# A scan kernel's chunk products on four quarters of the matmul array, with its state products and its levels issued by shape

## The reference, cut to what matters

```
def step(s, inp):
    r_t, w_t, k_t, v_t, kk_t, a_t = inp
    sa = jnp.einsum('bhvk,bhk->bhv', s, -kk_t)
    s = (s * w_t[:, :, None, :] + sa[..., None] * (kk_t * a_t)[:, :, None, :]
         + v_t[..., None] * k_t[:, :, None, :])
    return s, jnp.einsum('bhvk,bhk->bhv', s, r_t)
```

## Time and profile before

| | |
|---|---|
| median of 3 runs | 4100.36 us (4093.78 to 4100.76) |
| the profiled execution, its own time | 4094.72 us |
| its span, first to last instruction | 4092.9 us |
| mean granted clock of TensorE | 0.943 of full |
| the scan, from its first to its last instruction on PE | about 1131 to 2293 us |
| bodies with a solve and state steps, between starts of `begin0` | 17, from 1183 to 2253 us |

### The profile page before, as it was taken

The page is one execution under the profiler, slowest core; times in us unless marked ns, Lnnn a source line. Parts: engine busy times, 40 slices in busy tenths (PEclk is TensorE's granted clock), DMA queues, the critical chain, the costliest instruction groups (busy, mean ns, idle before and its releaser), DMA issues. The chain is left out here.

```text
span 4092.9 us, 93137 instructions
## 1 busy us (share of the span) xinstructions
PE 3684.4 (90%) x39677; PEld 3199.6 (78%) x39677; DVE 2350.2 (57%) x4331; ACT 1910.5 (47%) x2991; POOL 1215.6 (30%) x1222
## 2 busy tenths in 40 slices
PE   5699999999978898988989688897599999999997
PEld 2578888888767777777778588675499999999986
DVE  3236666640046766766667655343666666667676
ACT  3335666641145665665656444232244443444454
POOL 1223333331045555555553255101001010111102
PEclk7799999999989999999999799898699999999999
DMA  5235555542264454444442466343367676666786
GB/s 172 62 120 176 179 180 169 176 148 75 69 127 87 94 107 82 91 106 86 96 85 47 155 217 188 119 145 122 101 203 213 205 212 205 201 216 206 235 278 218
DMA packets 771394, 611.33 MB, mean 149 GB/s; under 512 B 267618, under 2 KB 698532, under 8 KB 769956
## 3 DMA queue, kind: packets, MB, share of 16 engines
q1 hardware_dynamic: 721828, 493.84, 42.2%
q0 software_dynamic: 22688, 80.75, 6.6%
q10 hardware_dynamic: 26464, 30.77, 2.5%
HBM read 443.62 MB, written 161.50 MB: 148 GB/s over the span
## 5 line engine op out<-in xcount | busy, mean ns | idle before, releaser
L579 PE MATMUL moe_h<-moe_xt_hi,moe_w_hi 128*128 128x256 f32 x2048 | 583.2, 285 | 7.9 <-DVE moe_w_lo L431 4.0
L431 DVE TENSOR_TENSOR moe_w_lo<-moe_w_lo_whole,moe_w_hi 128x2048 fp32r<-128x2048 f32 x254 | 446.3, 1757 | 243.4 <-ACT moe_w_hi L647 196.5
L579 PE MATMUL moe_h<-moe_xt_hi,moe_w_lo 128*128 128x256 f32 x2048 | 580.9, 284 | 0.0
L579 PE MATMUL moe_h<-moe_xt_lo,moe_w_hi 128*128 128x256 f32 x2048 | 580.9, 284 | 0.0
L1963 PE MATMUL inward_pp<-u_u_hi,inward_w_hi 128*128 128x512 f32 (+1 forms) x1360 | 527.9, 388 | 20.4 <-POOL inward_w_lo L2123 20.4
L1963 PE MATMUL inward_pp<-u_u_lo,inward_w_hi 128*128 128x512 f32 (+1 forms) x1360 | 516.3, 380 | 0.0
L1963 PE MATMUL inward_pp<-u_u_hi,inward_w_lo 128*128 128x512 f32 (+1 forms) x1360 | 516.0, 379 | 0.0
L579 PEld LDWEIGHTS moe_h<-moe_xt_hi,moe_w_hi 128*128 128x128 f32 x2048 | 394.1, 192 | 19.0 <-issue 5.9
L579 PEld LDWEIGHTS moe_h<-moe_xt_lo,moe_w_hi 128*128 128x128 f32 x2048 | 394.2, 192 | 3.6
L579 PEld LDWEIGHTS moe_h<-moe_xt_hi,moe_w_lo 128*128 128x128 f32 x2048 | 394.1, 192 | 0.0
L487 POOL DMA_INDIRECT scratch_x<-moe_ys,moe_who x30 | 86.1, 2870 | 867.0 <-DVE moe_ys L753 748.5
(11 more groups left out here) (386 smaller groups left out, 8929.7 us busy)
## 6 DMA issues: line engine op xcount, KB each, us to landing
moe_w_lo_whole<-in_moe_w SPq DMA_DIRECT2D x384, 512.0 KB, 5.1
scratch_ops<-inward_ops SPq DMA_DIRECT2D x72, 512.0 KB, 3.8
scan_by_parity<-scratch_ops SPq DMA_DIRECT2D x144, 192.0 KB, 6.4
inward_w_lo_whole<-in_w_in SPq DMA_DIRECT2D x38, 512.0 KB, 4.5
scan_aq<-scratch_ops SPq DMA_DIRECT2D x72, 256.0 KB, 4.9
scan_kb<-scratch_ops SPq DMA_DIRECT2D x36, 512.0 KB, 5.7
scratch_gates<-inward_out SPq DMA_DIRECT2D x64, 256.0 KB, 2.1
all_late<-in_w_mod POOLq DMA_DIRECT2D x32, 512.0 KB, 5.2
```

The source lines that it names most:

```text
L431: return nc.vector.tensor_tensor(x_lo, x, x_hi.bitcast(F32), ALU.subtract)
L579: mm = nc.tensor.matmul(hb[ft % 2][m][:, 0:CAP], w_, x_, start=(k == 0 and part == 0), stop=(k == KD - 1 and part == 2))
```

## The change

Four parts, all of the scan or of what feeds it.

1. **Products with B and K.** In `begin1` pair 0's products with B and pair 1's with K are issued in turn (`joint`), in `begin2` the other two. B's go from partitions h to output partitions h, K's from h to the other half, from a copy `over` of K, A and Q with the heads of a pair swapped, so that four matmuls of 64 rows by 64 columns lie on four quarters. `begin2` waits until DVE has taken out both products of `begin1`.
2. **State S.** K's products for both pairs and directions, then Q's, then B's, where before each direction of each pair had its own K, Q, B.
3. **Levels.** The products of both pairs, then the transpositions of both, where before pair 0 had both first.
4. **Layout.** A and Q of a chunk lie side by side in `ops`, with the decays behind, so that one transfer for each pair loads all that was three; `kb` is now `ob` (B alone), and `over` is loaded too, by two transfers for each pair. The decay is a column of this tile, and DVE multiplies by it one direction at a time (two TENSOR_SCALAR instructions for one TENSOR_TENSOR). H has two buffers for three, and H of level m waits for F of level m - 2. Some tiles move into constants that are no longer in use.

The core of the diff:

```diff
                     if own:
-                        for x in range(2):
-                            sp.dma_start(aq[u][:, it % 2, :, x, :], by_chunk(src[:, (6 + 2 * x) * G:(8 + 2 * x) * G])).then_inc(s_aq[u][it % 2], 16)
-                        sp.dma_start(till_end[u][:, it % 2, :], src[:, 10 * G:OPS]).then_inc(s_aq[u][it % 2], 16)
+                        sp.dma_start(aq[u][:, it % 2, :], src[:, AT_AQ:OPS]).then_inc(s_aq[u][it % 2], 16)
                     if rest:
-                        sp.dma_start(kb[u][:, :, :].rearrange("p x t -> p (x t)"), src[:, 2 * G:6 * G]).then_inc(s_kb[u], 16)
+                        sp.dma_start(ob[u][:, :], src[:, AT_B:AT_K]).then_inc(s_ob[u], 16)
                         for r, part in enumerate(HALVES):
                             for h, head in enumerate(HALVES):
-                                sp.dma_start(xp[u][part, :, h, :], by_chunk(src[head, 0:6 * G])[:, r::2, :]).then_inc(s_xp[u], 16)
+                                sp.dma_start(xp[u][part, :, h, :], by_chunk(src[head, 0:AT_AQ])[:, r::2, :]).then_inc(s_xp[u], 16)
+                        for part, head in zip(HALVES, HALVES[::-1]):
+                            sp.dma_start(over[u][part, :], src[head, AT_K:AT_END]).then_inc(s_over[u], 16)
 
             def reload(it):
                 for u in U:
@@ -2414,7 +2424,7 @@
             def reload_own(it):
                 for u in U:
                     PEc[u].wait(sp, "S3", it)
-                    DVc[u].wait(sp, "S3", it)
+                    DVc[u].wait(sp, "Sb3", it)
...
+            def beside(u, k, lhs, rhs, across):
+                for h, other in zip(HALVES, HALVES[::-1]):
+                    to = bank[u][2 + k // 4][other if across else h, k % 4 * P:(k % 4 + 1) * P]
+                    mm = nc.tensor.matmul(to, lhs[h, k * HD:(k + 1) * HD], rhs[h, k * P:(k + 1) * P], start=True, stop=True)
+                return mm
+
+            def joint(r, a):
+                it, b, half = a
+                uB, uK = (0, 1) if r == 1 else (1, 0)
+                for u in U:
+                    if r == 1:
+                        AC[u].wait(pe, "V", it)
+                    else:
+                        DV[u].wait(pe, EVICTED[FIRST_OF[u][0]][1] + "1", it)
+                pe.wait_ge(s_over[uK], 32 * it + 32)
                 for k in range(8):
-                    d, c = k // 4, k % 4
-                    for h in HALVES:
-                        moving = aq[u][h, a[1], k, :, :].rearrange("p x t -> p (x t)")
-                        mm = nc.tensor.matmul(bank[u][2 + d][h, c * P:(c + 1) * P], kb[u][h, first + d, c * HD:(c + 1) * HD], moving, start=True, stop=True)
-                PE[u].did(name, mm)
+                    mmB = beside(uB, k, ob[uB], aq[uB][:, b, :], False)
+                    mmK = beside(uK, k, over[uK], over[uK][:, 2 * G:], True)
+                PE[uB].did("B", mmB)
+                PE[uK].did("K", mmK)
 
             def begin(r, a):
...
+            def turn_inverse(u, m):
                 whole = W[u][:, :, :].rearrange("p d c -> p (d c)")
                 for pos in range(4):
...
@@ -2558,22 +2579,25 @@
                     for d, x in every:
                         h = HALVES[x]
                         mm = nc.tensor.matmul(sums[u][h, 1, d * HD:(d + 1) * HD], blk(Wf, d, x), X[u][h, d, :], start=True, stop=True)
+                elif step == "K":
+                    ACg.wait(pe, "ri"[u], 4 * it + c)
+                    DVc[u].wait(pe, f"Z{c}", it)
+                    for d, x in every:
+                        mm = nc.tensor.matmul(sum_of(d, x, WHOLE), both(byK, d, x), blk(V, d, x), start=(d == 0), stop=False)
+                elif step == "Q":
+                    for d, x in every:
+                        h = HALVES[x]
+                        mm = nc.tensor.matmul(sum_of(d, x, HALVES[1]), own_of(u, h, b, 4 * d + at[d], 1), S[u][h, c % 2, d, :], start=False, stop=False)
                 else:
-                    DVc[u].wait(pe, f"Z{c}", it)
-                    ACg.wait(pe, "ri"[u], 4 * it + c)
-                    for d in range(2):
-                        for x in range(2):
-                            nc.tensor.matmul(sum_of(d, x, WHOLE), both(byK, d, x), blk(V, d, x), start=True, stop=False)
-                        for x, h in enumerate(HALVES):
-                            nc.tensor.matmul(sum_of(d, x, HALVES[1]), aq[u][h, b, 4 * d + at[d], 1, :], S[u][h, c % 2, d, :], start=False, stop=False)
-                        for x, h in enumerate(HALVES):
-                            mm = nc.tensor.matmul(sum_of(d, x, WHOLE), both(byB, d, x), Z[u][h, d, :], start=False, stop=True)
-                PEc[u].did(f"{step}{c}", mm)
+                    for d, x in every:
+                        mm = nc.tensor.matmul(sum_of(d, x, WHOLE), both(byB, d, x), Z[u][HALVES[x], d, :], start=False, stop=(d == 1))
+                if step in "XZS":
+                    PEc[u].did(f"{step}{c}", mm)
 
             def states(at, c):
                 if c is not None and at in STATE_AT:
                     chunk, step = STATE_AT[at]
-                    for part in step:
+                    for part in ("KQS" if step == "S" else step):
                         for u in U:
                             state(u, chunk, part, c)
...
+                    product = FIRST_OF[u][r - 1]
+                    PE[u].wait(dve, product, it)
+                    second = lambda x: x[u][b][:, :, :, 1, :]
+                    for name, x, part, mask in ((("W0", four(W[u][:, :, :]), 0, "lev0"), ("Lb", second(byB), 1, "nincl")) if product == "B" else
+                                                (("La", four(La[u][b][:, :, :]), 0, "strict"), ("Lk", second(byK), 1, "incl"))):
+                        for d in U:
+                            pairs = bank[u][2 + d].rearrange("p (c x f) -> p c x f", x=2, f=HD)[:, :, part, :]
+                            D.did(f"{name}{d}", dve.tensor_tensor(x[:, d], pairs, masked(mask)[:, d], ALU.mult))
 
             def square(u, m, a):
                 it, b, _ = a
...
                     D.wait(dve, f"Ub{c}", it)
-                    gain = till_end[u][:, b, c:8 - c:7 - 2 * c].unsqueeze(2).broadcast_to([P, 2, HD])
-                    D.did(f"S{c}", dve.tensor_tensor(S[u][:, (c + 1) % 2, :, :], undecayed[u][:, :, :], gain, ALU.mult))
+                    for d, at in ((0, c), (1, 3 - c)):
+                        gain = aq[u][:, b, 4 * G + 4 * d + at:4 * G + 4 * d + at + 1]
+                        D.did(f"S{'ab'[d]}{c}", dve.tensor_scalar(S[u][:, (c + 1) % 2, d, :], undecayed[u][:, d, :], gain, None, ALU.mult))
 
             def taps(k):
                 if k > LAST_PIECE:
@@ -2951,9 +2974,12 @@
                         AC[u].wait(pool, "L", it)
                         if it:
                             PE[u].wait(pool, "F5", it - 1)
-                    elif m > 3:
-                        PE[u].wait(pool, f"F{m - 3}", it)
-                    PO[u].did(f"H{m}", pool.tensor_tensor(four(H[u][(m - 1) % 3][:, :, :]), four(L[u][:, :, :]), masked(f"lev{m}t"), ALU.mult))
+                    elif m == 2:
+                        if it:
+                            PE[u].wait(pool, "F4", it - 1)
+                    else:
+                        PE[u].wait(pool, f"F{m - 2}", it)
```

123 lines of the change are left out of this document (59 added, 64 removed).

## The result

The changed kernel is **slower**, by 1.6%: 4171.5 us in the median of 4 runs (4152.4, 4166.9, 4176.1 and one, disturbed, of 10637, which the ratio leaves out), against 4100.6 for the kernel before beside it; ratio 1.0156, 95% interval 1.0113 to 1.0200. The profiled execution took 4152.4 us (span 4150.5, mean granted clock 0.929). Forecast were 4010, in a range from 3950 to 4085, and 0.08 for slower.

The account below looks back on a forecast made before the run. PE leads, but DVE's share is high enough that the stretch decides. Stretches sum 3.9 + 0.9 + 1.3 - 1.0 + 0.3 = 5.4 us a body, 92 over 17, minus 2 elsewhere: profiled 4094.7 becomes 4005, median 4010; range 3950 to 4085.

Parts of the forecast that it names:

- The bank rule: Different row tiles cannot access one PSUM bank at once; rival: a joint place is no faster, 4076 us, chance 0.03.
- The first stretch: begin0 to begin1, 11.16 us: 3.9 us a body less, through fewer load issues and less work at half clock.
- three signs of being wrong: Two updates at 1.5 us or more, bodies' clock well under 0.95, or PE's busy time still filling the second stretch.
- DVE's list in the second stretch: begin1 to S of chunk 1, 18.26 us: DVE's instructions sum to 17.3, so only 0.9 us a body less.
- The third stretch: S of chunk 1 to F3, 16.43 us: 1.3 us a body less, between bounds 0 and 2.0.
- At no cost: H's third buffer: Levels: dropping it is free, since H4 and H5 wait for F2 and F3 8 us or more before being needed.
- the fourth stretch: F3 to F4, 6.36 us: 1.0 us a body more, since S ends sooner but DVE's chain stays.
- inward: Same elements in other strides, two more issues a group, at no cost; if DVE or SP were late, 11 us.
- Slower: DVE's two instructions: Rival on the state update: POOL holds up each instruction, 1.8 us for two instead of 0.8; 4144 us, chance 0.08.
- Levels: 1.2 us a body faster: Level products and transpositions grouped over both pairs: half the shape changes go, 0.2 us less each, 1.2 a body.
- the first solve and the last states together cost 2: Outside the 17 bodies: first solve and last states together lose 2 us against the 92 gained.
- The rival of the clock: Idle 2.5 us at begin2 lowers TensorE's clock for begin2, S, begin3; 3 us on the path, 4060 us, chance 0.15.

Follow-up runs that it names:

- h_early: Changed kernel with the H of levels 1 and 2 made ahead of W's unit diagonal instead of behind it; 4182.8 us, ratio 1.0204.
- thin_h: Changed kernel writing only the first of four chunks of each H from the third body on (inverses not the reference's); 4094.8 us, ratio 0.9989.
- b_thin_h: Kernel before, writing only the first of four chunks of each H from the third body on (inverses not the reference's); 4093.6 us, ratio 0.9996.
- b_h_two: Kernel before with two H buffers for each pair instead of three, nothing else; 4137.2 us, ratio 1.0084.
- b_ts: Kernel before with two TENSOR_SCALAR for each update of the states, nothing else; 4129.2 us, ratio 1.0067.
- own_h3: Changed kernel with B of both pairs, then K of both, from rows of their own, no swapped copy, three H buffers; 4115.8 us, ratio 1.0032.
- b_level: Kernel before with the change's order of levels alone (both pairs' products, then both pairs' transpositions); 4108.3 us, ratio 1.0017.
- after: The changed kernel itself, with all four parts of the change; 4171.5 us, ratio 1.0156.
- before: The kernel before the change, run beside the changed one; 4100.6 us.
- own_tt: own_h3 with one TENSOR_TENSOR for each update of the states instead of two TENSOR_SCALAR; 4049.0 us, ratio 0.9888.
- no_joint: Changed kernel without joint places: B of both pairs in begin1, K of both in begin2, K still from the swapped copy; 4140.0 us, ratio 1.0114.
- own_tt_pairs: own_tt with the levels in the old order, leaving only S by shape and the new operand layout; 4037.9 us, ratio 0.9867.
- joint_h3: Changed kernel with three H buffers for each pair, joint place and two TENSOR_SCALAR kept; 4161.9 us, ratio 1.0151.

## Why the prediction was wrong

**Right: PE's prices.** Places of 1.75 us each were forecast and S of 2.7; measured were 1.9 to the start of S and 2.76. "PE idle some 2.5 us before the second joint place, on DVE": 2.42; the evictions of both pairs end just before it starts, at about 1597.4. The bank rule of the Trainium skill (TensorEngine Tiling (Array Packing), Gotcha 1: PSUM Pressure), which the prediction set against the joint place, didn't show in these 1.9 us. The first stretch shrank by 6.5 us, not 3.9: the wait for A and Q went to 7.0, not 20, and the clock in it is 1.00 where it was 0.69. Of the three signs of being wrong one came, the clock of the bodies (0.89); two updates took 0.83 us, and PE is busy 14.5 of 21.8 us in the second stretch.

**The step that failed: DVE's list in the second stretch.** "runs `recur` and `series` for 4.17 before Z of chunk 1", and "It hides, by little". I took the durations of the trace as they stood and asked of POOL only whether H would be *there* in time, not beside *what* it would run. In the earlier trace rows H runs at 1573.91, beside evictions and updates, `recur` beginning at 1579.00; with W of pair 1 taken out last, H slides onto `recur`, and it doesn't quite hide either: pair 0's first H is done 15.0 us after `begin1`, not 13, and PE waits 0.8 us for pair 1's. 4.17 became 8.1 us, the stretch 21.8 instead of 17.3. Term by term, measured and forecast: 2.4 for 1.85 to the first eviction, 8.9 for 7.9 to the first update (the taps beside POOL's first addition take 2.97 us), 1.9 for 2.9 for the updates, 8.1 for 4.17, and 0.4 for 0.48. `h_early` shows that the long instructions follow H to its new place, `thin_h` and `b_thin_h` that with H cut the loss against the kernel before is gone.

**The third stretch, "1.3 less".** It is 3.8 longer, with 5.1 us the largest miss of the five; the second has 4.4. The bounds of 0 and 2.0 had no term for the clock. PE waits 3.4 us for Z just before the stretch, and in it the clock is 0.67 where it was 1.00: PE is busy 18.25 us for 14.30, though it has some 2.0 us less to do.

**The step "At no cost: H's third buffer".** The H are there in time, as I said; but POOL now writes them after F, at another time, and beside the recurrences. In the body above the fourth stretch, forecast 1.0 longer, is 1.6 longer and holds 3.1 us of POOL, the two H of level 5, where it held 1.2. By `b_h_two` the two buffers cost 34 us. `inward`, also taken at no cost, did cost nothing: the first L starts at 1121.6 to 1127.0 us in the 13 profiles with the new layout, at 1127.1 to 1131.4 in the six with the old one.

**The update, mis-sized.** "I take 0.8 for two": in the changed kernel it was 0.83, a good number by luck: H had left that place for another. It was the rival "Slower: DVE's two instructions", with its price of 1.8 for two, that had the mechanism: 1.28 in `b_ts`, 1.34 in `own_h3`, 2.52 in the body shown of it. I priced it only in the order of before, and it isn't what made the changed kernel slower: it is 16 us there (within the noise), 59 where H is at its old place.

**Levels: 1.2 us a body faster.** Measured alone it is 7 us slower. PE is busy 954 us in the bodies of `b_level`, for 962: 0.5 us a body less, not 1.2. That ScalarE's copy starts later I had written down; which wait gives the gain back stays open.

**"the first solve and the last states together cost 2".** The first solve alone took 17.7 us more. In `after` PE waits there 3.25 us for the swapped copy, 2.97 before the second joint place and 1.56 behind it for evictions; its first level starts 38.6 us after the first L, in `before` 25.5, in `own_tt` 28.5. In all kernels with the joint place the first solve is 69 to 71 us, whatever H, the update or the order of the loads do. Without it it is 51 to 57, but 62.5 in `no_joint`, which still loads the swapped copy: so some 5 us go to the copy (the two buffers differ too, but in `b_h_two` they cost the first solve nothing) and some 7 to the joint places.

**The rival of the clock** had the wrong place, but not too large a price. The clock fell, to 0.89 over the bodies, but in the body read at the wait for Z, not at `begin2`. At 0.89 for 0.95 some 8 us more of each body are at the lower level, an estimate from these two means, and that is worth up to 4 us where PE works through them; the rival had 3. As a cause by itself it fails: the bodies of `thin_h` have 0.90 and take 1073 us, 44 less than those of `after` and hardly more than the 1070 of before. The clock adds to what the waits cost; how much of the 47 us is its share no run separates.

How the 118 us from `own_tt_pairs` to the changed kernel divide, by the ratios, one step after the other: the levels' order 9, the joint place with its copy 65, two buffers and two updates together 45. Another order of the steps divides them otherwise, since they hide each other (`own_h3` to `joint_h3` is 49, not 65). Nor do the 65 us separate the copy from the joint place; but `no_joint` to `own_h3`, where both the copy and the two buffers go, is 34 us, as much as two buffers cost the kernel before alone.

## What to carry to other kernels

When a change reorders work, write down for each instruction of GpSimd what VectorE does beside it before and after, and mark which of VectorE's instructions touch SBUF alone: a move that is free by its waits can double a recurrence. A saving on a busy engine counts only in stretches where no other engine is at its limit; here PE's 62 us turned into idleness. Undo the parts singly and together: with H and the updates one alone gave 16 us, the other 2, both 45.
